# A planned attention and GLA layer on eight cores: narrower guards, paced transfers, a last tile with more banks, and small products at the start

## The reference

```
h    = rms_norm(x, g_pre);  proj = h @ w_in                 # D_IN = 5648 columns
# mixer A: 4 heads, two maps of 64; softmax(q k^T/8 - slope*dist), causal
oa   = softmax(map 0) @ v - lam * softmax(map 1) @ v
ya   = (rms_norm(oa, g_sub_a) * (1 - lam_init) * silu(za)) @ w_up_a
# mixer B: gated linear attention in chunks, 4 heads
ob   = gla(q_b * dk**-0.5, k_b, v_b, log_sigmoid(lr @ w_alpha + b_alpha) / 16)
yb   = (rms_norm(ob, g_sub_b) * silu(zb)) @ w_up_b
y    = sigmoid(gate_a) * ya + sigmoid(gate_b) * yb
out  = x + rms_norm(y @ w_out, g_post)
```

## Time and profile before

| | |
|---|---|
| median of 3 runs | 1318.84 us (1316.91 to 1324.17) |
| the profiled execution | 1318.94 us; span of its slowest core 1317.3 us |
| spans of the cores | 1307.8 to 1317.3 us |
| PE busy | 1217.8 us (92%) |
| PEld, DVE, ACT, POOL busy | 662.4, 737.6, 746.6, 193.6 us |
| HBM read, written | 173.06 MB, 32.51 MB |

### The profile page before, as it was taken

One profiled execution on the slowest core, in us unless ns is written; L12 is line 12 of the kernel. 1 busy time (PEld: TensorE's weight loads), 2 busy tenths in 40 slices (PEclk: granted clock), 3 DMA queues, 4 the chain that ended last, 5 costly groups with the idle time before them and its releaser, 6 DMA issues.

```text
span 1317.3 us, 27507 instructions; the slowest of 8 cores (1307.8 to 1317.3 us)
## 1 busy us (share of the span) xinstructions
PE 1217.8 (92%) x9379; PEld 662.4 (50%) x9551; DVE 737.6 (56%) x2228; ACT 746.6 (57%) x1066; POOL 193.6 (15%) x307
## 2 busy tenths in 40 slices
PE   5898899699999999999999999999999999999986
PEld 2445345345555454555555555555555555555532
DVE  4769777734667447563475534755346553474344
ACT  3656445254754457555666556775568668666511
POOL 1213001300222002110121101211012010021000
PEclk9899999899999999999999999999999999999988
DMA  8896799754593438543484333744327441343441
GB/s 242 272 308 203 228 285 296 194 189 146 166 266 103 135 136 232 163 141 134 137 240 129 113 129 137 240 130 113 129 105 208 157 117 66 136 138 105 145 176 67
DMA packets 115618, 222.40 MB, mean 169 GB/s; under 512 B 68176, under 2 KB 76816, under 8 KB 100496
## 3 DMA queue, kind: packets, MB, share of 16 engines
q1 hardware_dynamic: 115472, 220.54, 54.5%
HBM read 173.06 MB, written 32.51 MB: 156 GB/s over the span
## 4 chain that ended last, share of the span: by engine, by line
PE 82%; DVE 5%; DMA 5%; issue 4%; SPq 2%; ACT 1%; POOL 0%; DVEq 0%; POOLq 0%; ACTq 0%
PE ps_pg L528 59%; PE ps_acc L528 14%; PE ps_qk L974 8%; DMA sb_wbuf<-wsc 2%; DMA sb_KT<-w_in 1%; SPq L501 1%; DMA sb_xr<-x 1%; SPq L606 1%; DVE sb_otmp L1015 1%; DMA sb_KT<-w_up_a 0%; DVE sb_ste L907 0%; ACT sb_PT L981 0%; DVE sb_szB L705 0%; PE ps_pg L532 0%; DVE sb_tmp L1142 0%
## 5 line engine op out<-in xcount | busy, mean ns | idle before, releaser
L981 ACT ACTIVATE sb_PT<-ps_qk 128x1024 bf16<-128x1024 f32 (+2 forms) x445 | 411.9, 970 | 188.1 <-PE ps_qk L974 182.1
L528 PE MATMUL ps_pg<-sb_hT,sb_wbuf 128*128 128x512 bf16 x1542 | 406.5, 382 | 11.3 <-DMA sb_wbuf<-wsc 3.1
L528 PE MATMUL ps_acc<-sb_V,sb_PT 128*128 128x129 bf16 x3340 | 373.1, 220 | 6.9 <-ACT sb_PT L981 1.8
L528 PEld LDWEIGHTS ps_acc<-sb_V,sb_PT 128*128 128x128 bf16 x3340 | 259.4, 98 | 114.9 <-issue 17.1
L528 PE MATMUL ps_pg<-sb_wbuf,sb_hT 128*128 128x512 bf16 x851 | 226.0, 383 | 7.8 <-issue 2.4
L528 PEld LDWEIGHTS ps_pg<-sb_hT,sb_wbuf 128*128 128x128 bf16 x1616 | 149.2, 98 | 155.6 <-issue 28.5
L1087 DVE SCALAR_TENSOR_TENSOR sb_tmp<-sb_tmp,ps_pg 128x512 f32<-128x512 f32 x120 | 82.2, 686 | 200.1 <-PE ps_acc L528 136.5
L1063 ACT ACTIVATE sb_tmp<-ps_pg 128x512 f32<-128x512 f32 x120 | 71.7, 597 | 119.8 <-PE ps_pg L528 68.1
L974 PE MATMUL ps_qk<-sb_QT,sb_KT 64*128 64x256 bf16 (+1 forms) x1754 | 130.3, 267 | 5.6 <-ACT sb_PT L981 2.2
L528 PEld LDWEIGHTS ps_pg<-sb_wbuf,sb_hT 128*128 128x128 bf16 x896 | 82.1, 98 | 86.8 <-issue 20.8
L1026 POOL TENSOR_TENSOR sb_statE<-sb_statE,sb_mhalf 128x1 f32<-128x1 f32 x128 | 73.2, 580 | 316.4 <-DVE sb_statE L1024 303.6
(11 more groups left out here) (170 smaller groups left out, 1257.5 us busy)
## 6 DMA issues: line engine op xcount, KB each, us to landing
sb_wbuf<-wsc SPq DMA_DIRECT2D x97, 1024.0 KB, 6.0
sb_KT<-w_in SPq DMA_DIRECT2D x88, 256.0 KB, 7.6
sb_xr<-x SPq DMA_DIRECT2D x34, 512.0 KB, 6.1
sb_xa<-x SPq DMA_DIRECT2D x30, 512.0 KB, 7.3
out<-sb_xr SPq DMA_DIRECT2D x30, 512.0 KB, 4.8
wsc<-sb_wbuf SPq DMA_DIRECT2D x10, 1024.0 KB, 9.9
wsc<-sb_V SPq DMA_DIRECT2D x5, 1024.0 KB, 11.4
sb_KT<-w_out SPq DMA_DIRECT2D x16, 256.0 KB, 8.9
```

Source lines behind the costliest of these rows:

```text
L528: return P.op(_pe(n), lambda e: e.matmul(out=out_f(), lhsT=lf(), rhs=rf(), start=start, stop=stop, **kw), reads=reads, writes=writes, mode ...
L981: P.op({"act": (0.075 + width / 600.0, 0.1)}, lambda e: e.activation(out=PT[pt.i][:, :, 0:width], in_=qk[:, 2 * half:2 * half + 2, 0:width ...
```

## The change

- `EARLY` maps each pool to one key: an early operation becomes a reader only of the key of the pools that it touches (`w` to `vxdone`, `xa` to `xrdone`, `hb` to `ytdone`).
- `schedule` starts a transfer no earlier than 3 us (`BACKLOG`) before the modelled end of the transfers already planned.
- With `near`, 110 matmuls of a constant tile of ones with itself, 128 columns each, write one bank of `qk`, at the lowest priority; the opening's products on `qk1` come behind all of them. `ones` is written first on POOL.
- The sums of squares of mixer B write the keys `junkd0` to `junkd3`.
- In the last tile `ups` transposes the two later blocks into `qk` banks and puts the up products of the two branches into `acc0` and `acc1`.
- `stage_f` of the last tile is the new `end_f`: row blocks 0 and 1 sum into the four `qk` banks, parts 0 to 6 of both ahead of part 7 of either; block 2 uses `acc`, block 3 `pg`. The scale of the mean goes into the square, and L1144 and L1146 become one instruction. The last row block is stored in two halves.
- SP reads the flag and branches before the operation that waits for the stores.

```diff
+BACKLOG = 3.0
+EARLY = {"w": "vxdone", "xa": "xrdone", "hb": "ytdone"}
+WARM = 110
...
-        if self.early_key is not None and any(
-                isinstance(b, _Buf) and b.pool in ("w", "xa", "hb") for b in [k[0] if isinstance(k, tuple) else k for k in list(reads) + list(writes)]):
-            self.readers.setdefault("vxdone", []).append(o)
-            self.readers.setdefault("xrdone", []).append(o)
-            self.readers.setdefault("ytdone", []).append(o)
+        if self.early_key is not None:
+            for p in {b.pool for b in [k[0] if isinstance(k, tuple) else k for k in list(reads) + list(writes)] if isinstance(b, _Buf)}:
+                if p in EARLY:
+                    self.readers.setdefault(EARLY[p], []).append(o)
...
                     st = o.ready if o.ready > ef else ef
+                    if o.is_dma and st < dma_free - BACKLOG:
+                        st = dma_free - BACKLOG
...
+            if near:
+                small("pool", 128, lambda e: e.memset(ones[:], 1.0), [], ["ones"])
+                keep = P.stream
+                P.at(ntiles + 1, ntiles + 2, "warm")
+                for _ in range(WARM):
+                    P.op({"pe": (0.11, 0.17)}, lambda e: e.matmul(out=qk[:, 2, 0:128], lhsT=ones[:], rhs=ones[:], start=True, stop=True),
+                         reads=["ones"], writes=["qk1"], mode="full")
+                P.stream = keep
...
-                        b = P.buf("pg")
+                        if t == ntiles - 1 and a >= 2:
+                            b, src = f"qk{a - 2}", lambda a=a: qk[:, 2 * (a - 2), :].bitcast(BF16).rearrange("p (n c) -> p n c", c=128)
+                        else:
+                            b = P.buf("pg")
+                            src = lambda b=b: ptr(b)
...
-                    b = P.buf("pg")
+                    b = P.buf("pg") if t < ntiles - 1 or ntiles == 1 else f"acc{ab}"
...
+            def end_f(t, wo):
...
+                    if s < 2:
+                        homes = [(lambda j=j: qk[:, j, :], f"qk{j // 2}") for j in (2 * s, 2 * s + 1)]
+                    elif s == 2:
+                        homes = [(lambda j=j: acc[j][:, :], f"acc{j}") for j in range(2)]
+                    else:
+                        bs = [P.buf("pg") for _ in range(2)]
+                        homes = [(lambda b=b: pg[b.i][:, :], b) for b in bs]
...
+                def part(s, kcs):
+                    for hh in range(2):
+                        out_f, key = rows[s][5][hh]
+                        for kc in kcs:
+                            mm(out_f, lambda kc=kc, s=s: yT[:, kc, :][:, s * 128:(s + 1) * 128],
...
+                    P.op({"dve": _dve(1)}, lambda e, st=st: e.scalar_tensor_tensor(out=statF[st.i][:, 3:4], in0=statF[st.i][:, 0:1], scalar=EPS,
+                                                                                 in1=statF[st.i][:, 1:2], op0=ALU.add, op1=ALU.add),
...
+                for s in range(2):
+                    part(s, range(7))
+                for s in range(2):
+                    part(s, range(7, 8))
+                    close(s)
+                for s in range(2, 4):
+                    part(s, range(8))
+                    close(s)
...
                 far = e.value_load(flag[0:1, 0:1])
                 with e.If(far != 0):
+                    if name == "sp":
+                        quick[name](e, True)
...
+                if name == "sp":
+                    quick[name](e, True)
```

More of the change, by code:

```diff
@@ L341, in make, with body @@
             my_ops = [o for o in ops if o.eng == eng_name]
-            def body(e):
-                for o in my_ops:
+            def body(e, finish=False):
+                for o in my_ops[-1:] if finish else my_ops[:-1] if eng_name == "sp" else my_ops:
                     need = {}
@@ L492, in program @@
                 for nm in ([f"cst{i}" for i in range(12)] + [f"stg{i}" for i in range(NSTG)] + [f"wld{i}" for i in range(NW + NWX)] + [f"wst{i}" for i in range(NW + NWX)]
-                           + [f"xa{i}" for i in range(4)] + [f"xr{i}" for i in range(2)] + [f"sxr{i}" for i in range(2)] + [f"sxa{i}" for i in range(2)] + ["ko0", "ko1"]
+                           + [f"xa{i}" for i in range(4)] + [f"xr{i}" for i in range(2)] + [f"sxr{i}" for i in range(2)] + [f"sxa{i}" for i in range(2)] + ["ko0", "ko1", "sy0", "sy1"]
                            + [f"th{i}" for i in range(6)] + ["tk0", "tk1", "tb0", "tb1"] + [f"ta{i}" for i in range(4)]):
@@ L565, in program @@
                               ["block2z"], [f"block2{v}{m}"])
-                small("pool", 128, lambda e: e.memset(ones[:], 1.0), [], ["ones"])
             def v_ef(half):
@@ L918, in stage_gla @@
                             out=junkd[:, hd * 128:(hd + 1) * 128], in0=cum[:, oi, hd * 128:(hd + 1) * 128], scalar=1.0 / 128, in1=cum[:, oi, hd * 128:(hd + 1) * 128],
-                            op0=ALU.mult, op1=ALU.mult, accum_out=statB[st.i][:, hd:hd + 1]), reads=[f"cum{oi}"], writes=[(st, hd)])
+                            op0=ALU.mult, op1=ALU.mult, accum_out=statB[st.i][:, hd:hd + 1]), reads=[f"cum{oi}"], writes=[(st, hd), f"junkd{hd}"])
                     P.op({"dve": _dve(4)}, lambda e, st=st: e.tensor_scalar(out=statB[st.i][:, 4:8], in0=statB[st.i][:, 0:4], scalar1=EPS, scalar2=None,
@@ L1085, in ups @@
                     group(b, 4, [(wu, ab * 4 + kc) for kc in range(4)] + [f"{name}{a}" for a in range(4)],
-                          lambda kc, off=off, w=wu: wbuf[w.i][:, off + kc * 512:off + kc * 512 + 128], lambda kc, src=src: src[:, kc, :], after=keys)
-                    P.op({"dve": _dve(512)}, lambda e, b=b, ap=ap: e.scalar_tensor_tensor(out=ap(), in0=ap(), scalar=1.0, in1=pg[b.i][:],
+                          lambda kc, off=off, w=wu: wbuf[w.i][:, off + kc * 512:off + kc * 512 + 128], lambda kc, src=src: src[:, kc, :], after=keys, out_f=home)
+                    P.op({"dve": _dve(512)}, lambda e, home=home, ap=ap: e.scalar_tensor_tensor(out=ap(), in0=ap(), scalar=1.0, in1=home(),
                                                                                          op0=ALU.add, op1=ALU.mult), reads=[b] + keys, writes=keys)
@@ L1123, in stage_f @@
                     wo = [(lambda w=w: wbuf[w.i], [(w, k) for k in range(8)]) for w in (acquire(W_O), acquire(W_O + 1))]
+                if last:
+                    end_f(t, wo)
+                    return
                 for s in range(4):
@@ L1203, in program @@
                     stage_batt(t + 1, [])
-            P.op({"sp": (0.05, 0.0)}, lambda e: None, reads=[f"out{g}" for g in range(4 * ntiles)] + [f"wsc{c}" for c in range(NCHUNK)], writes=["end"])
+            P.op({"sp": (0.05, 0.0)}, lambda e: None, reads=[f"out{g}" for g in range(4 * ntiles)] + [f"out{4 * ntiles - 1}_{hh}" for hh in range(2)] + [f"wsc{c}" for c in range(NCHUNK)], writes=["end"])
             P.schedule()
@@ L1229, in body @@
                     full[name](e)
+                    if name == "sp":
+                        full[name](e, True)
+                if name == "sp":
+                    quick[name](e, True)
             return body
```

41 lines of the change are left out of this document (39 added, 2 removed).

## The result

The changed kernel takes 1300.88 us (median of 4 runs, 1300.25 to 1301.74), the one before on the same chip 1319.03 (1316.91 to 1324.17): a ratio of 0.9859, 95% interval 0.9837 to 0.9882. The forecast was 1305.0, the range 1293 to 1317. The cores differ by some 9 us from one another, and in each run another one is the slowest.

What follows compares the result with a forecast made beforehand. PE's own products were taken to bound the kernel from 264 to 1110 us, with gains only outside. On core 4, 5.8 + 3.4 + 3.7 + 1 = 13.9 off 1318.9 gave 1305.0 us, range 1293 to 1317.

Steps and rivals of the forecast that it cites:

- likeliest case: Whole kernel: the terms hold as forecast, 1305.0 us, its own range 1297 to 1311; chance 0.58.
- Guards by pool, 5.8: 222 to 264 us: x loads go early, PE's 8.54 us wait for the residual add goes, DVE takes 2.73 back.
- later planned transfers, 1: Transfers planned with at most 3 us queued: 0 from 264 to 1110, 1 us gained from 18 to 222.
- rival B: Up to 264 us: the new plan gives the gain back, x displaces weights, a loss of 3, 1314.8 us; chance 0.17.
- After the last attention, 3.4: Last stage, core 4: 3.4 from filled waits, 1.7 from the clock, less 1.7 for the banks; elsewhere 1.7 us.
- The `acc` banks were to cost 1.7: After the last attention: one bank per branch delays two groups of up products, 1.7 us of PE come later.
- The end, 3.7: After PE's last product: 0.67 us from one merged instruction and 3.0 from SP's flag read and branch moved earlier.
- the 3.0 for the branch: Program end: SP's flag read to drain runs beside the last store's landing, drain at 1314.0 instead of 1317.0, 3.0 us gained.
- Rival D: Program end: the time after the branch is SP's drain after a store, so it stays; 1307.5 us; chance 0.08.
- The constant's products, 0: Opening: 110 products of a constant gain 0 us, since DMA sets the pace there.
- Rival C: Weight loads planned just in time arrive late; nine 2.43 us waits cancel the gain, twelve give 1334.2 us; chance 0.08.
- E: Opening, 18 to 222 us: it moves too, gaining a third of PE's 21.3 idle us instead of 1; 1299.0; chance 0.09.

Runs made afterwards that it cites:

- experiments 2, 3 and 5: The changed kernel with the old guards (2), without the limit on planning ahead (3), with neither (5): 1310.3, 1310.0 and 1318.5 us (median of all four runs).
- experiment 4: The changed kernel with the old work for the last tile, SP's flag still read ahead of the last wait: 1305.4 us.
- experiment 8: The changed kernel with SP's flag read and branch before its last four stores instead of behind them: 1299.8 us.

## Why the prediction held, step by step

The time came 4.1 below the forecast, inside the likeliest case's own range. The sum was 13.9 on core 4; its profiled span fell by 17.5, the mean span by 17.6. The terms were less good than the sum, and that they came this near is in part luck: on core 4 the work up to the last attention product gained 6.3 (forecast 6.8), the work after it 9.0 (3.4), the end 2.2 (3.7).

**Guards by pool, 5.8, and later planned transfers, 1.** The wait, its cause (x planned behind a store that it does not need) and the place were right: the stretch from tile 2's to tile 3's norms is 2.7 shorter, up to tile 4's 6.9. (In the trace the store had landed at 235.7, 4.1 us before x's issue; in between SP issued transposes and other rows that the plan had set ahead of x.) The failed step is that I priced the two apart, and the second from "DMA share of 0.50, it rarely binds". By experiments 2, 3 and 5 they are worth 9.7 together and 2.9 if added one by one. The guards let x go early; without a limit the planner then issues it at 174.8 and something else is late. The limit orders waiting transfers by due time, but with the old guards x still waits for a store. My lower end for the guards, "delays what is behind it on SP's queue", is what happens without the limit, near to what rival B describes.

**After the last attention, 3.4 (others 1.7).** Core 4 gained 9.0, the mean 4.2; experiment 4, which loses 5.5 there, shows that all of it is this edit. Three sizes were off on core 4, and one term was missing. The `acc` banks were to cost 1.7: PE's first waits sum to 3.65 (2.93 + 0.72), against 3.57 before (0.75, 0.47, 2.35), so nothing, though on core 0, which never had the 2.35, they grew by 1.4 (2.05 to 3.42). Of the later waits, 4.8 with one of 0.37, I kept 1.0; none over 0.15 is left (on core 4 also because the weight landed earlier, experiment 4). The clock was put at 1.7, from one row of 31 products, and that was near: before, products ran at 1.2 GHz behind the waits of 2.35 and 2.43, those behind the 1.98 did not; after, only some behind the first waits do. By the intervals between products the lower clock cost 2.7 us before and 1.2 after, a gain of 1.5. Granted clock behind the 2.43 and behind the 1.98, before (columns as in the earlier trace rows; the clock is the 0.50 of the first row and the 1.00 of the second):

```profile
1278.00:1281.00 3.00, 3.00 (x9) 1.07 (x8) 0.00 (x0) 0.60 (x1) 0.00 (x0) 0.50 0.00 0
1292.00:1300.00 8.00, 7.95 (x36) 3.30 (x36) 3.63 (x8) 2.75 (x8) 0.55 (x1) 1.00 0.00 0
```

The missing term is what the rows hide: PE's busy time for the same 196 products fell by 4.1, and 2.6 of it are pauses between products too short to show as idle, since the recorded length of a pipelined product covers them. Twenty-one such pauses add up to 3.5 us before, five to 0.8 after; the up products' 0.97 to 1.0 instead of 0.86 per group is the plainest case. Which of the edits removed them (the `acc` banks, or the output products in between) was not tried.

**The end, 3.7.** Mean and core 4: 2.2. Of the merged instruction's 0.67 nothing came: from PE's last product to the end of the last store's issue it is 4.60, before 4.43, and with the old last stage (experiment 4) 4.42.

```profile
1292.28 0.15 DVE L1168 SCALAR_TENSOR_TENSOR sb_statF<-sb_statF 128x1 f32<-128x1 f32 x1
1292.35 0.68 DVE L1166 TENSOR_TENSOR sb_tmp<-ps_pg,sb_gpost 128x512 f32<-128x512 f32 x1
1292.95 2.06 DVE L1174 SCALAR_TENSOR_TENSOR sb_xa<-sb_tmp,sb_statF,sb_xa 128x512 f32<-128x512 f32 x3
```

DVE's last three L1174 (the scaling and residual add) start 0.67 after the merged L1168, but the first of them is the third row block's second half; the last block's two halves stand behind it. Of the 3.0 for the branch 2.3 came. From the start of the flag read to SP's next instruction behind the branch it is 3.74 us now (the read alone 0.79, before 0.47), against 3.03, and ends 0.6 behind the landing. So the step that put 1310.66 + 3.0 ahead of the landing was mis-sized, and the sign "within 4 us of that store's issue" failed narrowly (4.05 from the issue's end); experiment 8, with the branch out of the way, ends 0.5 earlier on average. Rival D is refuted: with the branch ahead of the stores the drain stands right behind the last wait (0.05 us), where before it came 2.46 us behind the branch with nothing left to wait for. The Trainium skill's rule that a taken branch to code not yet loaded waits for the fetch ("Runtime: NRT & Kernel Launch", Instruction fetch mechanics) agrees with the 2.46; the 108 ns for a compare-and-branch ("Advanced Engine Details and Errata", Control Flow Timing) are of the order of the branch's own 53 ns on SP and 72 ns on DVE and leave out what follows it.

**The constant's products, 0.** Right in size, wrong in reason. I had "no gain by 27 us, since DMA sets the pace"; the products after the 31 ran on at 24.90 without a wait, against 26.86 before, so the sign "still no gain by 27 us" failed. With or without the constant there is no wait for weights there now, since 22 pieces of `w_in` are issued ahead of the constants: the cover that I named is gone through another edit. What takes the gain stands at 45 us.

**Rival C** (what is planned late arrives late) is refuted: at a limit of 0.4 weights cost PE less than at 3.0 (core 4). **E**, an opening that moves too, shows at the first tile (2.3 us earlier) and is still there at the second (2.3); it is a third of the 7 us that E had, and more than half of it is the limit's (120.1 and 120.2 at the second tile without it).

Open: pair, last stage and end sum to 9.7 + 4.3 + 2.2 = 16.2 of 17.6; the other 1.4 no experiment isolates, and it is little more than the error of such a sum, whose terms have standard errors of 0.5 to 0.9 (the keys on `junkd` were not tried alone, nor the three guards one by one). And why 1.5 beats 3.0 by 7 is shown only in place (between the second and third tile, half lost by the fourth, and again by the sixth), not by a single transfer.

## What to carry to other kernels

Price edits to a plan's order as a set: two that free the same wait can be worth 0.5 and 2.4 us alone and 9.7 together, so try them in all four combinations before dropping one. A limit on how far ahead transfers are queued is a number to scan. Where a wait cannot be shortened, have independent products ready for it: on average over the cores the late weight landed as late as before, and the waits for it nearly went. And look at the intervals between products as well as at the idle time: short pauses hide in the busy time.

## What the runs showed of the hardware

Half the bytes did not land sooner: the two stores of 256 KB at the end took a median of 3.7 us from issue to landing, the 512 KB store just before them 3.4 (all three were issued within 1.4 us, so they may have been in each other's way).

The constant's products did not keep the clock up for long behind a wait. In the kernel without a limit they ended at 10 us, PE then waited 4.89, and 16 transposes took 1.86 us, the time at 1.2 GHz. In the changed kernel PE waited 3.56; half of the 16 transposes behind the wait still ran at 2.4 GHz (all 16 took 1.46 us), then the granted clock was 0.50 until 15.8. There ten and twelve more of the constant's products stand between the transposes, and the products behind them, from 18.22, run at 2.4 GHz from the first on.

Four loads of 16 KB (`w_alpha`) held SP's queue for 6.46 us in the opening before, where a 512 KB load took 0.43, and they stood ahead of pieces of the weights. One of them, the first, took 4.65 of that (from 10.47 on); the other three took 0.42 to 0.84 each, and in the changed kernel all four, issued from 29.41 on, took 2.08. So the loads' size and number are not the price; what held the first one no run here shows.
